# Encoder block in float32: the buffers that the stages share are placed first in SBUF, the lasting buffers above them

## The reference

```python
mod = silu(c) @ w_ada + b_ada                 # six vectors of 1024: shift, scale, gate, twice
h = rms_norm(x, norm1_gain) * (1 + sc1) + sh1
x = x + g1 * token_mixer(h)                   # h @ w_in (1024x6656), gated conv, banded attention, @ w_o
h = rms_norm(x, norm2_gain) * (1 + sc2) + sh2
a, b = split(h @ w_up)                        # 1024x5632
x = x + g2 * ((gelu(dwconv3(a) + bias) * b) @ w_down)   # 2816x1024
```

## The kernel before

| buffer | address before | address modulo 64 |
|---|---|---|
| `h_hi`, `h_lo`, `xT` | 16512, 32896, 49280 | 0 |
| `w_raw`, `w_hi`, `w_lo` | 65664, 82048, 98432 | 0 |
| `par` (744 bytes), `mod`, ..., `ident`, ... | 114816 to 119488 | 0 |
| `a_buf`, `b_buf`, `y_buf` | 119488, 123584, 127680 | 0 |
| `pad_f` (4112 bytes) | 131776 | 0 |
| shared region: start | 135904 | 32 |
| its `x_nat`, `ada0`, `kv_hi`, `kv_lo` | 135904, 152288, 187104, 203488 | 32 |
| its `merged`, `k_st`, `q_st`, `v_st` | 135904, 152288, 168672, 176864 | 32 |
| its `prob`, `pt_hi`, `pt_lo`, `ada`, `acc` | 191200, 203488, 207584, 211680, 219872 | 32 |
| its `g_hi`, `g_lo` | 135904, 180960 | 32 |
| end of the region | 226016 | |

## Time and profile before

### The profile page before, as it was taken

The page is one execution under the profiler, slowest core; times in us unless marked ns, Lnnn a source line. Parts: engine busy times, 40 slices in busy tenths (PEclk is TensorE's granted clock), DMA queues, the critical chain, the costliest instruction groups (busy, mean ns, idle before and its releaser), DMA issues.

```text
span 835.5 us, 10295 instructions
## 1 busy us (share of the span) xinstructions
PE 786.8 (94%) x3661; PEld 645.8 (77%) x3661; DVE 531.8 (64%) x725; ACT 373.5 (45%) x661; POOL 361.1 (43%) x177
## 2 busy tenths in 40 slices
PE   3789889999999999989998899999999999999997
PEld 2568767788788878878888788888888888887886
DVE  4646778559755975597737788888888888000000
ACT  7536546644674467456434544443334443112220
POOL 3536332433343334323943444444555555444340
PEclk9799999999999999999999999999999999999999
DMA  9913534144414441433132133333332222323311
GB/s 306 356 47 116 187 102 151 51 158 141 151 55 158 141 151 55 152 126 126 51 114 88 51 102 100 100 100 100 100 100 88 85 86 79 101 89 114 124 48 40
DMA packets 83275, 95.97 MB, mean 115 GB/s; under 512 B 2674, under 2 KB 77610, under 8 KB 83242
## 3 DMA queue, kind: packets, MB, share of 16 engines
q1 hardware_dynamic: 79018, 93.44, 33.7%
q10 hardware_dynamic: 4224, 2.10, 0.9%
HBM read 93.43 MB, written 2.10 MB: 114 GB/s over the span
## 4 chain that ended last, share of the span: by engine, by line
PE 77%; DVE 16%; ACT 3%; issue 2%; SPq 1%; DMA 1%; DVEq 0%; ACTq 0%
PE bank L781 24%; PE bank L783 24%; PE bank L782 24%; DVE acc L1209 4%; PE bank L934 2%; PE bank L906 2%; DVE a_buf L1297 1%; DVE bank L1121 1%; DVE sm L1259 1%; DVE prob L1252 1%; PE bank L917 1%; DVE pt_lo L1273 1%; DVE h_lo L1428 1%; DVE pad_f L1289 1%; ACT prob L628 1%
## 5 line engine op out<-in xcount | busy, mean ns | idle before, releaser
L420 POOL TENSOR_TENSOR w_lo<-w_raw,w_hi 128x1024 fp32r<-128x1024 f32 x122 | 311.6, 2569 | 405.1 <-ACT w_hi L500 401.7
L781 PE MATMUL bank<-h_hi,w_hi 128*128 128x512 f32 (+1 forms) x792 | 309.1, 390 | 16.0 <-DVE h_lo L1142 10.5
L783 PE MATMUL bank<-h_hi,w_lo 128*128 128x512 f32 (+1 forms) x792 | 306.3, 387 | 0.0
L782 PE MATMUL bank<-h_lo,w_hi 128*128 128x512 f32 (+1 forms) x792 | 306.1, 387 | 0.0
L781 PEld LDWEIGHTS bank<-h_hi,w_hi 128*128 128x128 f32 x792 | 150.3, 190 | 48.4 <-DVE h_lo L1142 7.3
L783 PEld LDWEIGHTS bank<-h_hi,w_lo 128*128 128x128 f32 x792 | 150.3, 190 | 30.3
L500 ACT ACTIVATE w_hi<-w_raw 128x1024 fp32r<-128x1024 f32 x122 | 124.7, 1052 | 106.6 <-PE bank L783 106.5
L782 PEld LDWEIGHTS bank<-h_lo,w_hi 128*128 128x128 f32 x792 | 150.5, 190 | 28.1
L781 PE MATMUL bank<-g_hi,w_hi 128*128 128x512 f32 x176 | 69.9, 397 | 0.0
L783 PE MATMUL bank<-g_hi,w_lo 128*128 128x512 f32 x176 | 69.8, 397 | 0.0
L782 PE MATMUL bank<-g_lo,w_hi 128*128 128x512 f32 x176 | 69.5, 395 | 0.0
(11 more groups left out here) (170 smaller groups left out, 948.1 us busy)
## 6 DMA issues: line engine op xcount, KB each, us to landing
w_raw<-in_w_in_dram SPq DMA_DIRECT2D x23, 1024.0 KB, 5.1
w_raw<-in_w_up_dram SPq DMA_DIRECT2D x22, 1024.0 KB, 5.1
ada<-in_w_ada_dram SPq DMA_DIRECT2D x32, 512.0 KB, 5.9
ada<-in_w_ada_dram SPq DMA_DIRECT2D x32, 256.0 KB, 7.1
w_raw<-in_w_down_dram SPq DMA_DIRECT2D x8, 1024.0 KB, 5.0
w_raw<-in_w_o_dram SPq DMA_DIRECT2D x4, 1024.0 KB, 5.0
w_raw<-in_w_down_dram SPq DMA_DIRECT2D x4, 768.0 KB, 4.2
x_nat<-in_x_dram SPq DMA_DIRECT2D x4, 512.0 KB, 5.1
```

The source lines that it names most:

```text
L420: pool.tensor_tensor(w_lo[:, n % 2, u], w_raw[:, n % 2, :, u * P:(u + 1) * P], w_hi[:, n % 2, u], SUB).then_inc(lo_ready, 1)
L781: pe.matmul(dst, w_h, rhs_hi, start=first, stop=False)
L782: pe.matmul(dst, w_h, rhs_lo, start=False, stop=False)
L783: return pe.matmul(dst, w_l, rhs_hi, start=False, stop=last)
```

## The change

No instruction, wait, loop or load is added, removed or reordered; only the addresses differ. `start`, `mixer` and `channel` are opened first, then a buffer `union` of 90112 bytes (the largest of the three, `2 * FT * S` floats) holds their region, and all lasting buffers follow above it.

```diff
+        start = ExitStack()
+        x_nat = sb("x_nat", [P, NB, D], into=start)
...
+        start.close()
+        mixer = ExitStack()
...
+        mixer.close()
+        channel = ExitStack()
+        g_hi = sb("g_hi", [P, FT, S], f32r, into=channel)
+        g_lo = sb("g_lo", [P, FT, S], f32r, into=channel)
+        channel.close()
+        sb("union", [P, 2 * FT * S])
 
         h_hi = sb("h_hi", [P, KT, S], f32r)
...
-        start = ExitStack()
...
-        mixer.close()
...
-        channel.close()
```

More of the change, by code:

```diff
@@ L107, in sem @@
             return ctx.enter_context(nc.semaphore(name))
+        start = ExitStack()
+        x_nat = sb("x_nat", [P, NB, D], into=start)
+        ada0 = sb("ada0", [P, RING, 2, 2, PC], into=start)
+        acc0 = sb("acc0", [P, 2 * PC], into=start)
+        kv_hi = sb("kv_hi", [P, KT, 2 * PC], f32r, into=start)
+        kv_lo = sb("kv_lo", [P, KT, 2 * PC], f32r, into=start)
+        start.close()
+        mixer = ExitStack()
+        merged = sb("merged", [P, KT, S], into=mixer)
+        k_st = sb("k_st", [P, 2, KV, S], f32r, into=mixer)
+        q_st = sb("q_st", [P, HG, S], f32r, into=mixer)
+        v_st = sb("v_st", [P, NB, KV, 2, HD], f32r, into=mixer)
+        bias = sb("bias", [P, HG, BAND], into=mixer)
+        prob = sb("prob", [P, 2, HG, BAND], into=mixer)
+        pt_hi = sb("pt_hi", [P, 2, HG * P], f32r, into=mixer)
+        pt_lo = sb("pt_lo", [P, 2, HG * P], f32r, into=mixer)
+        ada = sb("ada", [P, 2, D], into=mixer)
+        acc = sb("acc", [P, D], into=mixer)
+        mixer.close()
[4 more added lines that the diff above has]
+        sb("union", [P, 2 * FT * S])
         h_hi = sb("h_hi", [P, KT, S], f32r)
@@ L158, in encoder_block @@
         k_n = spare[:, NB * PC:3 * NB * PC].rearrange("p (b j o d) -> p b j o d", b=NB, j=KV, o=2)
-        channel = ExitStack()
-        g_hi = sb("g_hi", [P, FT, S], f32r, into=channel)
-        g_lo = sb("g_lo", [P, FT, S], f32r, into=channel)
-        channel.close()
         par_rows = w_raw[:, 1, :, :].rearrange("p k n -> p (k n)")
```

## The result

The changed kernel takes 834.06 us in the median of 13 runs (828.91 to 835.5), the kernel before 836.11 us in 13 runs beside it (833.37 to 843.04). The ratio is 0.9942, with a 95% interval of 0.9921 to 0.9963: 0.6% faster, under the 1% that three runs of this kernel tell from no change, but clear of it with this many runs. The profiled execution took 834.06 us, its span is 832.2 us, 3.3 us less than before.

What follows compares the result with a forecast made beforehand. PE was taken to bound the kernel, with 77% of the chain of waits. Gains of 3.3 + 0.65 + 0.25 + 0.15 = 4.35 us took the median from 835.43 to 831.1 us, range 827.5 to 836.0.

Steps and rivals of the forecast that it cites:

- PE's pace: Matmuls of 512 columns: 226.7 ns a step with h moving, 233.3 with g, 233.8 with k_st; the region's operands reach h's pace.
- Down projection 3.3 us: Last stage: 528 matmuls each 6.6 ns faster, less 0.2 us for run-ins; gain 3.3 us, bounds 3.0 to 3.5.
- Output projection 0.65 us: 72 k_st matmuls gain 0.5 us, h behind them 0.15 us, 256 columns nothing; bounds 0.4 to 0.75 us.
- the run-in: Output projection: after k_st gives way to h, some nine matmuls take 231.1 ns before 226.7; its loss was counted 0.15 us.
- The alignment to 64 bytes: Shared region goes from 32 to 0 modulo 64, giving its operands h's pace; chance 0.76, 831.1 us.
- the size of 1/32: The 6.6 ns excess is 1/32 of 213.3 ns: a misaligned 512-float row has 33 pieces of 64 bytes, not 32.
- The mixer 0.25 us: Value matmuls and 384-column scores gain 0.4 to 0.8 us on PE; half of 0.5 counted, bounds 0 to 0.8.
- The start 0.15 us: 96 matmuls moving kv would gain 0.63 us if all counted; 0.15 us taken, bounds 0 to 0.6.
- Nothing from DVE, ACT, POOL and DMA: Everything else touching the region: 0, bounds -0.6 to +0.6 us, and DMA packets 0, bounds -0.3 to +0.3.
- The height case: Rival: SBUF above some byte is read slower, so moved h loses; chance 0.11, of which 0.06 near 842.7 us.
- The case of the run-in: Rival: h's run-in in the mixer vanishes too, some 1100 matmuls gaining up to 2.5 ns; 828.3 us, chance 0.05.
- The case of nothing: Rival: the longer step belongs to the stages, or 16-byte cachelines make placement free; time stays 835.4 us, chance 0.08.

Runs made afterwards that it cites:

- f2: The changed kernel with 32 empty bytes ahead of everything, all buffers keeping their places to one another; 0.9978 of the time of before.
- f3: The changed kernel with 128 empty bytes ahead of w_raw, so the weights lie 128 bytes further from h, g and k_st; 840.93 us in one run.
- f1: The kernel before with 928 empty bytes ahead of the shared region, which then begins high, at 136832; 0.9976 of the time of before.
- g3: The kernel before with 160 empty bytes ahead of g_hi and g_lo alone, kv, k_st and pt staying as before; 0.9962 of the time of before.
- g4: The kernel before with 160 empty bytes ahead of the whole shared region, buffer order kept; 0.9943 of the time of before, median 830.64 us.
- e3: The kernel before with h_hi, h_lo and xT moved by 32 bytes; 1.0117 of the time of before.
- g2: The changed kernel with weights starting 16 bytes into their buffers: weights less h 16, less g and k_st 240, modulo 256; 841.8 us in one run.
- e4: The changed kernel with 1920 empty bytes ahead of everything, so region and h begin at multiples of 2048; 0.9962 of the time of before.
- g1: The changed kernel with gaps so that weights less h is 224, less g and k_st 32, modulo 256; 846.45 us in one run.

## Why the prediction was right, and what it had wrong

The forecast was 831.1 us and 0.5% less; measured were 834.06 us and 0.58% less. The time lies above the bounds of the sum (828.8 to 832.9) and inside the range; the gain of 4.35 us lies between the 2.05 us of the medians and the 4.8 us of the means. The part on PE's pace was right, the reason given for it was wrong, and that the number came out in spite of it was luck. Point by point:

- *PE's pace is what counts, and the slow step is that of the shared region's operands.* Right. The step of g went from 233.3 to 226.7 ns, that of `k_st` from 233.8 to 226.7, that of h stayed.
- *Down projection 3.3 us.* Measured 3.3 us (127.1 to 123.8).
- *Output projection 0.65 us, 256 columns nothing.* Measured 0.60 us inside the stage, and the run-in at the change from `k_st` to h is gone, as counted. That a gain on PE here shortens the whole isn't borne out by the pair of profiles: the second norm behind it takes 0.6 us more.
- *The alignment to 64 bytes is the reason, and the size of 1/32 speaks for it.* Wrong, and this is the step of the reasoning that failed: "so the step follows the moving operand". It follows the pair of moving operand and weights. Before, only the moving operand changed inside the unit of the earlier trace rows, so those rows show that its place matters but not to what it must stand in relation. f2 (all at 32 modulo 64, 226.7 ns) and f3 (all multiples of 128, 232.2 ns) deny the alignment outright, and the 1/32 was a coincidence: the steps at other distances are 228.3, 228.9 and 232.2 ns. The forecast came out because the region's new beginning, 16512, is by construction the old place of `h_hi`, so every pair got the distance that the pair of h and `w_hi` had.
- *The mixer 0.25 us, from values and scores.* The scores gained nothing: their weights (`q_st`) lie in the same region as `k_st`, at a distance of 16384, 0 modulo 256 before and after, and four of 384 columns take 122.29 - 121.58 = 0.71 us in the changed kernel against 0.70 in the earlier trace rows. The values gained about half of the 0.46 us counted. Four of them take 118.83 - 117.92 = 0.91 us against 0.93 in the earlier trace rows; over the steps under 245 ns of all of them the mean with `pt_hi` moving goes from 233.8 to 226.6 ns, with `pt_lo` it stays (232.3 and 233.3). This is more than the table can explain. Their own weights (`v_st`) are at a distance of 26624 from `pt_hi`, 0 modulo 256 in both kernels. Where `pt_hi` is the last of the four, the load that runs beside it is already that of `w_hi`, whose distance went from 160 to 0; but the first of the four gains as well, and the load beside it is that of `v_st`. The table holds for long rows of one pair; what sets the step in groups of four stays open.

```profile
117.92 0.39 PE L937 MATMUL bank<-pt_hi,v_st 128*128 128x512 f32 x1
...
118.61 0.39 PE L937 MATMUL bank<-pt_hi,v_st 128*128 128x512 f32 x1
118.83 0.39 PE L784 MATMUL bank<-h_hi,w_hi 128*128 128x512 f32 x1
```

```profile
121.58 0.87 PE L909 MATMUL bank<-k_st,q_st 128*128 128x384 f32 x4
122.29 0.40 PE L784 MATMUL bank<-h_hi,w_hi 128*128 128x512 f32 x1
```

- *The start 0.15 us.* The pair of `kv` and h had a distance of 160 before and has 0 now, and nine steps in a row show the faster step: (43.07 - 41.03)/9 = 226.7 ns. How much of it reaches the end can't be read from runs whose start differs by as much by itself.

```profile
41.03 0.39 PE L784 MATMUL bank<-kv_hi,h_hi 128*128 128x512 f32 x1
...
43.07 0.39 PE L784 MATMUL bank<-kv_hi,h_hi 128*128 128x512 f32 x1
```

- *Nothing from DVE, ACT, POOL and DMA.* Right: 684 and 752 ns as before, DVE busy for 531.7 us against 531.8.
- *The rivals.* The height case is denied by f1, g3 and g4, where the region is high and fast. Its price was well worked, though, for the thing that really can go wrong: e3 costs 1.2% because the 2232 matmuls that move h take a slow step. The case of the run-in is denied too: the twelve matmuls with h moving behind the values take 121.58 - 118.83 = 2.75 us in the changed kernel, 229.2 ns each, and took 121.22 - 118.46 = 2.76 us before; over the 960 steps of the mixer in which h follows h the mean went from 229.1 to 228.5 ns, 0.6 ns where the rival counted 2.5. A run-in after a switch remains there, at a distance of 0, and has no explanation. The case of nothing, with cachelines of 16 bytes in the Trainium skill (SBUF — State Buffer, Specifications (TRN2)), is denied by the steps: 16 bytes off the good distance costs 6.6 ns in g2, so a whole number of such lines doesn't make a place free. The same page of the Trainium skill says also (Who interferes with whom) that PE has two SBUF read ports, for the moving operand and for the weight load, and calls them independent. A step that depends on the distance between the two operands fits badly with an independence in time, at the upper clock at least.

What stays open: why a distance of 0 is the good one, why 192 and 240 are in between, and what in the memory has a period of 256 bytes. The experiments give the steps, not the circuit. That the two reads of PE meet in the memory is the simplest account, and it was only argued.

The time of single experiments also isn't settled to the microsecond. f1 and f2 have all the steps of the changed kernel and ratios of 0.9976 and 0.9978, g4 has 0.9943; the lengths of the output and the down projection agree within 0.1 us in all three and the changed kernel, and the rest lies in the start, the mixer and the second norm, as below.

## What to carry to other kernels

Where PE runs long rows of 512 float32 columns without a gap, try the moving operands and the weights that meet them at the same place modulo 256 bytes. Small buffers placed between large ones shift everything behind them: here `pad_f` (4112 bytes) by 32 modulo 256, and `mod`, `amp`, `c_act`, `sink_b` and `sm` (832 bytes in all) by 64, while `par`, which takes 768, shifts nothing. 160 empty bytes repaired it. Read the step from start to start for each pair of moving operand and weights, some ten matmuls behind a switch: two steps for the same form at the same clock are a sign of placement. And before a placement is called aligned, move both partners together and each alone, since a comparison in which only one moves can't tell a relation from a place.

## What the runs showed of the hardware that was not expected

The step at the upper clock depends on the distance between the two operands, from 226.7 to 234.4 ns for 512 columns, while for 256 columns nothing showed (120 ns in the earlier trace rows, at distances of 0 and 160). At the lower clock, 1.2 GHz, it was 425 to 430 ns for either pair, which is 512 columns at one a cycle. Half of that, 213.3 ns, is an estimate for 2.4 GHz, and even the best step is 13 ns over it.

The executions of one kernel fall into groups: those of the changed kernel are five from 828.91 to 830.42 and eight from 833.47 to 835.5 us. The traces show one place where they part. In the profile of the changed kernel, a DVE instruction of the mixer begins 0.04 us before a POOL instruction and takes 3.50 us; PE waits 3.14 us for its successor and then runs at the lower clock (timeline of all engines; the mark in brackets is the wait and its releaser):

```profile
104.83 3.50 DVE L1212 SCALAR_TENSOR_TENSOR acc<-ada,c_act,acc 128x1024 f32<-128x1024 f32 x1
104.87 5.68 POOL L423 TENSOR_TENSOR w_lo<-w_raw,w_hi 128x1024 fp32r<-128x1024 f32 x2 [7.50 <-ACT w_hi L503]
...
109.00 1.42 PE L909 MATMUL bank<-k_st,q_st 128*128 128x384 f32 x4 [3.14 <-DVE prob L1255]
...
110.21 0.63 PE L784 MATMUL bank<-h_hi,w_hi 128*128 128x512 f32 x1
```

In the profile of g4 the same two begin 0.06 us apart, again DVE first. DVE now takes 1.29 us, POOL a little more than above (5.83 us for its two), and PE waits 0.93 us:

```profile
104.23 1.29 DVE L1210 SCALAR_TENSOR_TENSOR acc<-ada,c_act,acc 128x1024 f32<-128x1024 f32 x1
104.29 5.83 POOL L421 TENSOR_TENSOR w_lo<-w_raw,w_hi 128x1024 fp32r<-128x1024 f32 x2 [7.51 <-ACT w_hi L501]
```

```profile
106.19 1.12 PE L907 MATMUL bank<-k_st,q_st 128*128 128x384 f32 x4 [0.93 <-DVE prob L1253]
```

The two meet like this in all fourteen profiles, POOL 0.04 to 0.06 us behind DVE. In six of them (before, the changed kernel, e3, e4, g1, g3) DVE takes 3.49 or 3.50 us, in the other eight 1.28 or 1.29: a few hundredths of a microsecond go with a difference of 2.2 us on DVE. The stretch from 100 to 120 us has 73 matmuls at a mean clock of 0.91 in the changed kernel and 90 at full clock in g4, some 4 us of work at this kernel's step of 0.23 us. From the first scores to the output projection the changed kernel takes 315.7 us, g4 311.9.

That is about what parts the two groups, and as much as the change brought: a profile of one execution must be compared by stages, not by its span. But the meeting alone doesn't sort the executions. f1 and f2 have the short form, and their profiled executions took 833.3 and 835.07 us: they lose at the start, where the first scores begin at 92.0 and 92.8 us against 89.7 in g4, and f2 in the second norm too. What parts the groups in the runs without a profile stays open.
